# Pooling's running sums made per tile inside the projection, and loads reordered, in a hybrid decoder step

## The reference

```
p = x @ w_in                       # 1024 -> q 512 | k 512 | v 512 | forget logits 8 | pooling channels u 512
logf = log_sigmoid(f_logit + b_f);  c = cumsum(logf)
att  = softmax(q.k/8 + c[t] - c[s], causal) @ v
for g, w in enumerate((2, 4, 8, 16)):            # 4 groups of 128 channels
    pooled[g] = (sum of the last w rows of u[g]) / min(pos + 1, w) - u[g]
    mixed[g]  = (pooled[g] @ w_pool[g]) * pool_scale[g]
x1 = LayerNorm(alpha * x + concat(att, mixed) @ w_out)
x2 = LayerNorm(alpha * x1 + conv-FFN(x1))
```

## Time and profile before

| what | before |
|---|---|
| median of 3 runs | 3571.09 us (3564.25 to 3575.71) |
| profiled execution | 3569.61 us, its span 3567.9 us |
| busy in the span | PE 3188.2 us (89%), DVE 2104.7 (59%), ACT 1747.0 (49%), POOL 689.7 (19%) |
| projection | from the start to about 490 us |
| merged stage | about 490 to 597 us |
| attention | from about 597 us |
| mean granted TensorE clock | 0.954 of full speed |

### The profile page before, as it was taken

The page is one execution under the profiler, slowest core; times in us unless marked ns, Lnnn a source line. Parts: engine busy times, 40 slices in busy tenths (PEclk is TensorE's granted clock), DMA queues, the critical chain, the costliest instruction groups (busy, mean ns, idle before and its releaser), DMA issues. The chain is left out here.

```text
span 3567.9 us, 58096 instructions
## 1 busy us (share of the span) xinstructions
PE 3188.2 (89%) x20080; PEld 2501.6 (70%) x20080; DVE 2104.7 (59%) x3645; ACT 1747.0 (49%) x3493; POOL 689.7 (19%) x1197
## 2 busy tenths in 40 slices
PE   6999945888887996999999999899999999999867
PEld 5999943776766885777667777677776677777633
DVE  3222226777775654666676666766666776655645
ACT  2111102666665112466545666546665556665445
POOL 0101010000000102223233333223332333322000
PEclk9999976999999997999999999999999999999979
DMA  4443463232222346567786676776777876757575
GB/s 155 121 128 112 118 169 112 48 84 60 48 48 87 124 145 209 184 203 240 261 284 242 210 241 230 274 281 225 238 238 244 280 272 218 239 185 265 178 279 203
DMA packets 283548, 667.50 MB, mean 187 GB/s; under 512 B 56328, under 2 KB 135880, under 8 KB 274768
## 3 DMA queue, kind: packets, MB, share of 16 engines
q1 hardware_dynamic: 191479, 365.39, 32.3%
q0 software_dynamic: 87744, 283.71, 23.0%
q10 hardware_dynamic: 4032, 14.68, 1.1%
HBM read 592.78 MB, written 71.53 MB: 186 GB/s over the span
## 5 line engine op out<-in xcount | busy, mean ns | idle before, releaser
L1409 PE MATMUL F_ps_u<-X_x_hi,F_w_hi 128*128 128x512 f32 x1408 | 576.2, 409 | 7.2 <-DVE F_w_lo L1651 7.2
L1411 PE MATMUL F_ps_u<-X_x_hi,F_w_lo 128*128 128x512 f32 x1408 | 556.1, 395 | 0.0
L1410 PE MATMUL F_ps_u<-X_x_lo,F_w_hi 128*128 128x512 f32 x1408 | 555.4, 394 | 0.0
L1651 DVE TENSOR_TENSOR F_w_lo<-X_raw,F_w_hi 128x512 fp32r<-128x512 f32 x470 | 321.4, 687 | 396.1 <-ACT F_w_hi L1549 395.4
L1841 POOL DMA_DIRECT2D F_kin<-cache_k x512 | 278.7, 544 | 684.6 <-DVE F_kt L1705 496.9
L1549 ACT CAST F_w_hi<-X_raw 128x512 fp32r<-128x512 f32 x470 | 287.7, 615 | 228.0 <-PE F_ps_y L1411 101.9
L1705 DVE STREAM_TRANSPOSE F_kt<-F_kin 128x1024 f32<-128x1024 f32 x256 | 303.2, 1222 | 68.4 <-PE F_ps_t L1465 53.2
L1867 POOL DMA_DIRECT2D F_vin<-cache_v x512 | 282.9, 553 | 300.5 <-issue 176.0
L1409 PEld LDWEIGHTS F_ps_u<-X_x_hi,F_w_hi 128*128 128x128 f32 x1408 | 268.6, 191 | 98.4 <-issue 33.8
L1409 PE MATMUL F_ps_y<-F_w_hi,F_g_hi 128*128 128x512 f32 x704 | 295.8, 420 | 37.3 <-DVE F_w_lo L1651 37.3
L1411 PEld LDWEIGHTS F_ps_u<-X_x_hi,F_w_lo 128*128 128x128 f32 x1408 | 267.8, 190 | 58.2
(11 more groups left out here) (292 smaller groups left out, 6251.2 us busy)
## 6 DMA issues: line engine op xcount, KB each, us to landing
F_kin<-cache_k POOLq DMA_DIRECT2D x512, 256.0 KB, 3.7
F_vin<-cache_v POOLq DMA_DIRECT2D x512, 256.0 KB, 4.5
X_raw<-w_up_t SPq DMA_DIRECT2D x118, 512.0 KB, 5.0
X_raw<-w_down SPq DMA_DIRECT2D x117, 512.0 KB, 5.3
F_raw<-w_down SPq DMA_DIRECT2D x59, 512.0 KB, 5.3
F_raw<-w_up_t SPq DMA_DIRECT2D x58, 512.0 KB, 4.8
S_raw<-w_up_t SPq DMA_DIRECT2D x22, 1024.0 KB, 9.5
sc_qk<-A_qk SPq DMA_DIRECT2D x16, 1024.0 KB, 5.7
```

What stands on the lines that cost most here:

```text
L1409: nc.tensor.matmul(out, a_hi, b_hi, start=first, stop=False)
L1410: nc.tensor.matmul(out, a_hi, b_lo, start=False, stop=False)
L1411: return nc.tensor.matmul(out, a_lo, b_hi, start=False, stop=last)
L1651: nc.vector.tensor_tensor(w_lo[:, q % 4, :], raw[q // 2 % RAW][:, q % 2 * 512:(q % 2 + 1) * 512], w_hi[:, q % 4, :].bitcast(F32), ALU.subt ...
```

## The change

In the projection `ut` gets a halo of 16 columns ahead of its 128. ScalarE writes the turned u behind the halo. After group 1 of the next tile VectorE makes the window sums of the tile (`window_sums`): four additions by doubling, each over all groups that still need it, for tile 0 four multiplications with `cnt`, four subtractions into `pooled`, and a copy of the last 16 columns of `ut` into the halo. What is stored to the scratch tensor `uT` is now `pooled`. SyncE loads x of tile t + 2 at the beginning of its iteration t, ahead of that tile's stores, and stores `pooled` after q and k. `c_cnt` is loaded in the projection, ahead of the weights.

In the merged stage the long additions are gone; VectorE makes those of the new tokens ahead of `operands_of_decode` (the transposes of `ncs` and the block-diagonal queries), and TensorE runs the 4 x 5 matmuls ahead of the decode logits (`new_keys`). SyncE loads `pooled` (4 MB) last of the first loads; the 12 loads of the heads and the 8 copies come after the stores of `aug`; the store of the block-diagonal queries comes after `load_forget`. `c_cnt` is not loaded here. In the attention TensorE waits for `both` in the first `turn_back`.

```
 # projection, SyncE
             for t in range(TILES):
                 row, rows = prow[:, t % 2, :], slice(t * P, (t + 1) * P)
+                if t + 2 < NT1:
+                    load(t + 2)
                 evacuated(sp, NG * t + 4, p_act, p_dve)
...
-                sp.wait_ge(hi_out, t + 1)
-                sp.dma_start(sc["uT"][:, :, rows]..., ut[:, :, :]).then_inc(u_stored, 16)
                 sp.wait_ge(lo_out, t + 1)
                 sp.dma_start(sc["qk"]...).then_inc(qk_stored, 16)
-                if t + 2 < NT1:
-                    load(t + 2)
+                sp.wait_ge(pooled_ready, t + 1)
+                sp.dma_start(sc["uT"][:, :, rows]..., pooled[:, :, :]).then_inc(u_stored, 16)
 # projection, ScalarE
-                    act.wait_ge(u_stored, 16 * t)
+                act.wait_ge(ut_read, t + 1)
 # projection, VectorE
+            def window_sums(t):
+                dve.wait_ge(hi_out, t + 1)
+                n, link = HALO + P, Link(dve, sums)
+                link.enter(4 * t + (1 if t else 0))
+                src = ut
+                for k in range(G):
+                    sh, lo = 1 << k, 2 * (1 << k) - 1
+                    dst = wa if k % 2 == 0 else wb
+                    link(nc.vector.tensor_tensor(dst[:, k:, lo:n], src[:, k:, lo:n], src[:, k:, lo - sh:n - sh], ALU.add))
+                    src = dst
+                if t == 0:
+                    dve.wait_ge(cnt_in, 16)
+                    for g in range(G):
+                        dst = wa if g % 2 == 0 else wb
+                        last = nc.vector.tensor_tensor(dst[:, g, HALO:HALO + MAXW], dst[:, g, HALO:HALO + MAXW], cnt[:, g, :], ALU.mult)
+                    link(last)
+                else:
+                    dve.wait_ge(u_stored, 16 * t)
+                for g in range(G):
+                    dst = wa if g % 2 == 0 else wb
+                    last = nc.vector.scalar_tensor_tensor(pooled[:, g, :], dst[:, g, HALO:], 0.5 ** (g + 1), ut[:, g, HALO:],
+                                                          ALU.mult, ALU.subtract)
+                last.then_inc(pooled_ready, 1)
+                dve.wait_ge(pooled_ready, t + 1)
+                nc.vector.tensor_copy(ut[:, :, 0:HALO], ut[:, :, P:]).then_inc(ut_read, 1)
...
+                    if g == 1 and t:
+                        window_sums(t - 1)
 # merged stage, SyncE
-            sp.dma_start(cnt[:, :, :], io["c_cnt"]).then_inc(consts, 16)
...
-            sp.dma_start(uT[:, :, MAXW:], sc["uT"].rearrange("g p t -> p g t")).then_inc(u_in, 16)
...
-            for h in range(2):
-                load_head(sp, sc, persist, h)
-            for s in range(NB):
-                sp.dma_start(sc["vgrp"][s], ...).then_inc(q_stored, 16)
+            sp.dma_start(pooled[:, :, 0:SEQ], sc["uT"].rearrange("g p t -> p g t")).then_inc(u_in, 16)
...
                 sp.dma_start(sc["aug"][:, k, :]..., ch[:, k, :]).then_inc(aug_stored, 16)
-            sp.wait_ge(qbd_ready, 1)
-            sp.dma_start(sc["qbd"]...).then_inc(q_stored, 16)
+            for h in range(2):
+                load_head(sp, sc, persist, h)
+            for s in range(NB):
+                sp.dma_start(sc["vgrp"][s], ...).then_inc(q_stored, 16)
             sp.wait_ge(aug_stored, 64)
             sp.wait_ge(ones_set, 2)
             for h in range(2):
                 load_forget(sp, sc, persist, h)
+            sp.wait_ge(qbd_ready, 1)
+            sp.dma_start(sc["qbd"]...).then_inc(q_stored, 16)
 # merged stage, VectorE, for each group
-                    nc.vector.tensor_tensor(dst[:, lo:n], src[:, lo:n], src[:, lo - sh:n - sh], ALU.add)
...
-                link(nc.vector.tensor_tensor(src[:, MAXW:2 * MAXW], src[:, MAXW:2 * MAXW], cnt[:, g, :], ALU.mult))
-                nc.vector.scalar_tensor_tensor(pooled[:, g % 2, 0:SEQ], src[:, MAXW:n], 0.5 ** (g + 1), ...)
...
+                dve.wait_ge(pooled_ready, g + 1)
+            operands_of_decode()
 # merged stage, TensorE
             for g in range(G):
                 pe.wait_ge(pooled_ready, g + 1)
+                pe.wait_ge(u_in, 16)
...
+            new_keys()
 # attention, TensorE
             def turn_back(n):
+                if n == 0:
+                    pe.wait_ge(c_in, 32)
...
-            pe.wait_ge(c_in, 32)
             for r, j in parts_of(0):
                 logits(0, r, j)
```

More of the change, by code:

```diff
@@ L116, in stage_project @@
         vcat = m.sb("vcat", [P, H, 2, HD])
-        ut = m.sb("ut", [P, G, P])
+        HALO = MAXW
+        ut = m.sb("ut", [P, G, HALO + P])
+        wa, wb = m.sb("wa", [P, G, HALO + P]), m.sb("wb", [P, G, HALO + P])
+        pooled = m.sb("pooled", [P, G, P])
+        cnt = m.sb("cnt", [P, G, MAXW])
         stp = m.sb("stp", [P, PW])
@@ L141, in stage_project @@
             m.sem(n) for n in ("l_summed", "after_pe", "after_read", "w_ready", "w_stored"))
+        cnt_in, sums, ut_read, pooled_ready = m.sem("cnt_in"), m.sem("sums"), m.sem("ut_read"), m.sem("pooled_ready")
         SPAN = 4
@@ L149, in _ @@
             sp.dma_start(xin[:, :], io["x_prompt"][0, 0:P, :]).then_inc(x_in, 16)
+            sp.dma_start(cnt[:, :, :], io["c_cnt"]).then_inc(cnt_in, 16)
             sp.dma_start(ids[:, :], io["page_rows"]).then_inc(pages_in, 16)
@@ L182, in _ @@
                              qk[:, :, :, :].rearrange("p a c t -> p (a c) t")).then_inc(qk_stored, 16)
-                if t + 2 < NT1:
-                    load(t + 2)
+                sp.wait_ge(pooled_ready, t + 1)
+                sp.dma_start(sc["uT"][:, :, rows].rearrange("g p t -> p g t"), pooled[:, :, :]).then_inc(u_stored, 16)
                 if t % SPAN == SPAN - 1:
@@ L305, in turned_out @@
                     act.wait_ge(qk_stored, 16 * t)
[L306 removed]
+                act.wait_ge(ut_read, t + 1)
                 for j in range(2):
                     nc.scalar.copy(qk[:, 2 * j, :, :].rearrange("p c t -> p (c t)").bitcast(F32R), ps_t[:, j, :])
[L309 removed]
+                nc.scalar.copy(ut[:, :, HALO:], ps_t[:, 2, :].rearrange("p (c t) -> p c t", c=G)).then_inc(hi_out, 1)
             x_out(0)
@@ L466, in stage_gates_pool @@
         ones = m.sb("ones", [P, P])
-        uT = m.sb("uT", [P, G, MAXW + SEQ])
+        pooled = m.sb("pooled", [P, G, SEQ + S])
         tot = m.sb("tot", [P, P])
@@ L590, in _ @@
             nc.vector.transpose(kT[:, :, :, :], ks[:, :, :].rearrange("p g (f t) -> p g f t", t=32))
[L591 to L600, removed]
@@ L601, in _, with operands_of_decode @@
-            last.then_inc(qbd_ready, 1)
-            dve.wait_ge(u_in, 16)
-            n = MAXW + SEQ
-            for g in range(G):
[L606 to L610, removed]
+            def operands_of_decode():
+                dve.wait_ge(ncs_in, 32)
+                nc.vector.transpose(ncT[:, :, :], ncs[:, :, :]).then_inc(kT_ready, 1)
+                dve.wait_ge(qT_ready, 1)
+                dve.wait_ge(qbd_zero, 1)
+                for b in range(4):
+                    for g in range(2):
+                        part = slice(b * 32, (b + 1) * 32)
+                        last = nc.vector.tensor_copy(
+                            qbd[part, 4 * g:4 * g + 4, :, b, :].rearrange("p s f q -> p f s q"),
+                            qT[part, g, :, :].rearrange("p f (s q) -> p f s q", s=4))
+                last.then_inc(qbd_ready, 1)
@@ L675, in _ @@
                     n = 512 if k < 4 else S
-                    last = nc.tensor.matmul(ps_m[:, k, 0:n], wp[:, g, :], pooled[:, g % 2, k * 512:k * 512 + n],
+                    last = nc.tensor.matmul(ps_m[:, k, 0:n], wp[:, g, :], pooled[:, g, k * 512:k * 512 + n],
                                             start=True, stop=True)
                 last.then_inc(mixed_ps, 1)
+            new_keys()
         @block.gpsimd
```

52 lines of the change are left out of this document (24 added, 28 removed).

## The result

The changed kernel takes 3522.9 us (median of 4 runs, 3517.6 to 3523.7); the kernel before beside it 3570.2 us. The ratio is 0.9865, with a 95% interval of 0.9846 to 0.9883: 47 us faster. The forecast was 3529 us. The profiled execution's span fell from 3567.9 to 3522.0 us, by 45.9 us.

The account below looks back on a forecast made before the run. It took TensorE to bound the projection and an in-order DMA queue to delay the merged stage: -16.5 + 0.6 + 0 - 23.7 + 0 - 2.3 = -41.9 us, from 3571.1 to 3529 us, range 3509 to 3547.

Parts of the forecast that it names:

- The x load: Projection: x issued a tile ahead removes TensorE's waits for x but the very first, -16.5 us.
- `cnt` ahead of the weights: Projection start: one more DMA issue delays the weights TensorE waits for, +0.6 us.
- The window sums: Projection: 4.0 us of VectorE a tile, covered by its idle time, 0 on the path.
- the prediction's rule: Projection: a tile would pay the excess of VectorE's work over about 13 us of cover.
- The merged stage: Merged stage: last scaling ends at 567.5 in place of 591.2, set by group 0's store landing behind the queue, -23.7 us.
- The constants 0.6 us sooner: Merged stage start: without the cnt load constants come 0.6 us sooner, but VectorE still ends with GpSimd's fill, 0.
- `both`: Attention start: TensorE waits for `both` later and starts with the barrier, -2.3 us.
- the stores would overtake the heads: Rival, merged stage: stores of `mixed` don't wait for the head loads, 3512 us; 15%.
- The moved backlog: Rival, merged stage: heads and stores come one after another, the stage gives only 8 us, 3545 us; 15%.
- VectorE as the bound: Rival, projection: window sums at 17 us a tile make VectorE the bound, 3593 us; 3%.
- a gain given back: Rival: x stalls turn into equal waits and the backlog only changes place, 3563 us; 4%.

Follow-up runs that it names:

- e4: The changed kernel with a buffer of `mixed` for each of the four groups, so ScalarE waits for no store to land: 3519.1 us, ratio to before 0.9848.
- both edits together: The changed kernel with four buffers of `mixed` and attention head 1's operands loaded in the attention: 3501.2 us, ratio to before 0.9792.
- e3: The changed kernel with the 12 head loads and copies of v back right behind the load of `pooled`: 3517.6 us, ratio to before 0.9856.
- e2: The changed kernel with x of tile t + 2 loaded last in SyncE's iteration, behind the store of `pooled`: 3602.9 us, ratio to before 1.0094.

## Why the prediction was right

**The x load: right in mechanism, too small in size.** Forecast -16.5, measured 1.30 us in each of 15 tiles, -19.5. The wait's row shows the time in which TensorE did nothing; but matmuls overlap (each lasts 0.35 us and the next starts 0.19 us after it), and behind a wait this overlap is lost once. The mean idle of 1.1 us cost 1.3. One tile shows it: in the kernel before the transposes start 1.33 us after the start of the matmul ahead of them, 0.98 of them idle, in the changed kernel 0.19.

**`cnt` ahead of the weights: not seen.** Forecast +0.6. The first projection matmul starts at 15.31 us, earlier than the 16.01 of before. The first tile's end lies between 74.1 and 77.6 us in the ten kernels with this load, at 75.7 and 76.9 in the two without, which hides 0.6. It came 1.1 us earlier in the changed kernel than in the one before; these are in the -20.5, and no edit is shown to have made them.

**The window sums: right.** 3.34 us a tile under a cover of some 13 us; `x_rest`, forecast 0.3 us late in every fourth tile, was not late. With the additions made fourfold (some 10 us a tile) they cost nothing, eightfold (some 19 us) 155 us; the cover ends between the two. Beyond it the price is higher than the prediction's rule has it, 9.5 us a tile where the excess over 13 is 6.

**The merged stage: right in its steps, 2.5 us too hopeful.** `ncs` is issued at 20.9 and VectorE finds it there when it asks, at 28.5; the store of group 0 lands at 67.7 us into the stage (forecast 65), the last scaling ends at 79.4 (77.5), and from there to the attention it is 6.4 us (5.8). TensorE's fall to the low clock ahead of group 3 was in the sum. What was not is that groups 1 and 2 run at the high clock, with turns of 6.65 us in place of 9.4; it changed nothing, as they end in the wait for the store.

**The constants 0.6 us sooner: rightly put at nothing, but hardly tested.** The changed kernel shows the same 2.85 us, ended with GpSimd's fill (476.66 + 3.50 = 480.16). But the constants were there only 0.16 us sooner in the stage (VectorE's first instruction behind them starts at 475.26 - 469.53 = 5.73 us, before at 495.92 - 490.03 = 5.89):

```profile
476.66 3.50 POOL L711 MEMSET X_x_lo<- 4x4096 f32 x1
...
477.40 2.85 DVE L465 TENSOR_SCALAR B_lp<-B_ex 128x136 f32<-128x136 f32 x1 [0.38 <-ACT B_ex L657]
```

**`both`: right.** TensorE starts with the barrier, 0.04 us after SyncE:

```profile
555.38 0.45 PE L824 MATMUL C_ps_s<-H_ks,H_qs 128*128 128x128 f32 x1 [6.25 <-PEq L65]
```

**The rivals.** That the stores would overtake the heads is refuted for this queue: 3 MB taken from ahead of them brought the first landing 16.3 us forward, and in e4 the stores ready since 503 to 524 us went out one behind the other from 525 on. The moved backlog as a whole (3545) overestimated the stores: in line they follow each other every 3.3 to 3.9 us (e4 and both edits together), not every 4.5, and only the landing of group 0's held up a turn: group 3's scaling is released by TensorE. VectorE as the bound and a gain given back are refuted by the projection, where no wait came in the place of x's.

**The total: nearer than its parts.** The shares were -20.5, -21.2 and -2.6 where -15.9, -23.7 and -2.3 were forecast, so errors of 4.6 and 2.5 us partly cancel. The rest of -1.7 us is not explained by any step: from the first logits to the next stage the attention takes 525 to 532 us over all the kernels here whose attention is the same, in no order that follows the edits.

## What to carry to other kernels

A queue served in order is a resource with a length (here 3 MB of it were 16 us): ask what lies ahead of each store that somebody waits for, and the reorder that pays is the one that takes bytes from ahead of it or takes the waiter off it; moving a hold from one DMA to another pays nothing where nothing on the path waits for either (e3). When a stage-long computation is cut into tiles and put under another stage's matmuls, its own cost matters little while its place in the order does: here the same sums ahead of one load cost 80 us (e2). And an idle row understates what a stall costs TensorE: here 1.1 us idle a tile cost 1.3, and 7.2 cost 9.5.

## What the runs showed of the hardware

The loads into 64 partitions ran at about half the rate of those into 128: 215 GB/s for the head operands (a mean over 29 us at a DMA share of 1.01, with the copies of v in it) against 343 for `pooled` (a mean over 12.5 us; 428 from 480 to 485 us). The Trainium skill (SBUF — State Buffer, Door 1: The DMA port swizzle) says that the first 64 partitions reach only 8 of the 16 ports; the rows agree, for loads into the lower and the upper 64 partitions mixed. No run takes this apart from what else differs, as 512 KB a load against 4 MB.

A DMA's issue is not free of the queue: SyncE was held for 26.77 us at a 2 KB store behind the heads and the copies of v, and for 15.04 us at the first store of `mixed`, while in the changed kernel the twelve head loads ahead of it were issued in 0.6 us each. What of the queue it is that fills, bytes or pieces, the runs don't show.

A stall of about 8 us brought TensorE's granted clock to 0.50 (1.2 GHz) and the next 4 us of full work ran there; with waits of up to 4.1 us a tile (e2) the mean from 100 to 440 us was 0.96, and with waits of 1.1 us (the kernel before) it was 1.00.
